# Two output projections with the high and the low part of the activations in one 512-column product

## What is computed

```python
for i in range(DEPTH):                       # 2 layers: RG-LRU mixer, then GLA mixer
    h = rmsnorm_2(x, norm_g[i, 0]) * (1.0 + sc_m) + sh_m
    y = rglru_mixer(h, ...) if i == 0 else gla_mixer(h, ...)    # ends in  ... @ w_out   (1024 x 1024)
    x = x + gt_m * rmsnorm_2(y, norm_g[i, 1])
    h = rmsnorm_2(x, norm_g[i, 2]) * (1.0 + sc_f) + sh_f
    y = conv_ffn(h, ...)                     # ends in  ... @ w_down  (2816 x 1024)
    x = x + gt_f * rmsnorm_2(y, norm_g[i, 3])
```

## Time and profile before

| | |
|---|---|
| median of 3 runs | 1930.6 us (1929.88 to 1931.36) |
| profiled execution, its time | 1930.98 us |
| profiled execution, its span | 1929.2 us |
| instructions | 30067 |
| PE busy | 1847.6 us, 96% of the span |
| DVE busy | 1439.3 us, 75% |
| ACT busy | 887.6 us, 46% |
| HBM traffic | 157 GB/s on average |

### The profile page before, as it was taken

The page is one execution under the profiler, slowest core; times in us unless marked ns, Lnnn a source line. Parts: engine busy times, 40 slices in busy tenths (PEclk is TensorE's granted clock), DMA queues, the critical chain, the costliest instruction groups (busy, mean ns, idle before and its releaser), DMA issues.

```text
span 1929.2 us, 30067 instructions
## 1 busy us (share of the span) xinstructions
PE 1847.6 (96%) x11558; PEld 1619.9 (84%) x11558; DVE 1439.3 (75%) x2531; ACT 887.6 (46%) x1523; POOL 0.2 (0%) x4
## 2 busy tenths in 40 slices
PE   5899999999999999999999999999999999999997
PEld 2688887767888887988878999987999979989997
DVE  5548866558789897797866887676888778768863
ACT  3322223456232333443456455574655355546552
POOL 0000000000000000000000000000000000000000
PEclk9999999999999999999999999999999999999999
DMA  9333222011767777443222996443556924225552
GB/s 343 101 92 105 88 88 66 23 34 57 250 233 255 242 240 260 127 142 126 88 68 66 308 311 211 132 143 110 196 177 237 331 73 146 88 92 193 191 164 82
DMA packets 242909, 302.78 MB, mean 157 GB/s; under 512 B 6080, under 2 KB 224448, under 8 KB 242256
## 3 DMA queue, kind: packets, MB, share of 16 engines
q1 hardware_dynamic: 242768, 300.87, 47.1%
HBM read 299.79 MB, written 1.05 MB: 156 GB/s over the span
## 4 chain that ended last, share of the span: by engine, by line
PE 81%; DVE 8%; ACT 6%; issue 2%; SPq 1%; DMA 1%; DVEq 0%; ACTq 0%
PE bank L514 25%; PE bank L515 24%; PE bank L516 24%; DVE w_lo L1713 1%; ACT w_hi L1095 1%; PE bank L763 1%; DVE work L2150 1%; ACT work L1081 1%; PE bank L947 1%; PE bank L751 1%; PE bank L734 1%; PE bank L492 1%; PE bank L860 1%; DMA arena<-in_w_mod 1%; DVE arena L1781 1%
## 5 line engine op out<-in xcount | busy, mean ns | idle before, releaser
L514 PE MATMUL bank<-h_hi,w_hi 128*128 128x256 f32 (+2 forms) x2800 | 893.5, 319 | 27.5 <-DVE h_lo L1659 11.2
L515 PE MATMUL bank<-h_lo,w_hi 128*128 128x256 f32 (+2 forms) x2800 | 882.2, 315 | 0.0
L516 PE MATMUL bank<-h_hi,w_lo 128*128 128x256 f32 (+2 forms) x2800 | 881.6, 315 | 0.0
L1713 DVE TENSOR_TENSOR w_lo<-ring,w_hi 128x1024 fp32r<-128x1024 f32 (+2 forms) x444 | 500.3, 1135 | 232.9 <-ACT w_hi L1095 227.1
L514 PEld LDWEIGHTS bank<-h_hi,w_hi 128*128 128x128 f32 x2800 | 532.1, 190 | 78.9 <-ACT h_hi L1175 17.2
L516 PEld LDWEIGHTS bank<-h_hi,w_lo 128*128 128x128 f32 x2800 | 532.9, 190 | 35.5
L515 PEld LDWEIGHTS bank<-h_lo,w_hi 128*128 128x128 f32 x2800 | 531.3, 190 | 35.2 <-issue 0.7
L1095 ACT ACTIVATE w_hi<-ring 128x1024 fp32r<-128x1024 f32 (+2 forms) x444 | 434.4, 985 | 183.9 <-PE bank L516 152.3
L1081 ACT ACTIVATE work<-bank 128x512 f32<-128x512 f32 (+1 forms) x150 | 73.4, 506 | 306.6 <-PE bank L516 262.1
L514 PE MATMUL bank<-arena_r,w_hi 128*128 128x256 f32 (+2 forms) x464 | 154.0, 332 | 3.5 <-issue 1.9
L1081 ACT ACTIVATE arena<-bank 128x256 f32<-128x256 f32 (+4 forms) x113 | 51.4, 455 | 219.3 <-PE bank L516 156.9
(11 more groups left out here) (241 smaller groups left out, 1568.8 us busy)
## 6 DMA issues: line engine op xcount, KB each, us to landing
ring<-in_w_in SPq DMA_DIRECT2D x86, 1024.0 KB, 5.4
arena<-in_ada_w_t SPq DMA_DIRECT2D x96, 512.0 KB, 6.2
ring<-in_ffn_w_up SPq DMA_DIRECT2D x44, 1024.0 KB, 5.1
ring<-in_w_branch SPq DMA_DIRECT2D x32, 512.0 KB, 4.8
arena<-in_w_mod_t SPq DMA_DIRECT2D x32, 512.0 KB, 5.5
ring<-in_ffn_w_down SPq DMA_DIRECT2D x16, 1024.0 KB, 5.5
ring<-in_gla_w_in SPq DMA_DIRECT2D x12, 1024.0 KB, 5.5
ring<-in_w_out SPq DMA_DIRECT2D x8, 1024.0 KB, 5.2
```

Source lines behind the costliest of these rows:

```text
L514: pe.matmul(out, ws[0][:, k, :], hi, start=start, stop=False)
L515: pe.matmul(out, ws[0][:, k, :], lo, start=False, stop=False)
L516: return pe.matmul(out, ws[1][:, k, :], hi, start=False, stop=stop)
L1713: step(nc.vector.tensor_tensor(w_lo[u % PARTS][:, 0:nk, :], src, w_hi[u % PARTS][:, 0:nk, :].bitcast(F32), ALU.subtract), f"lo {u}", *(["u ...
```

## The change

High and low activations, two tensors before, become halves of one (`h_both`, and `ff_both` for the input tiles 16 to 21 of the down projection), so that one access pattern names both parts of a tile: 2 x 256 columns. `wide_products` replaces `three_products` in the four products named above. Its first product multiplies the high weight with both parts in 512 columns, which fill the whole bank: columns 0 to 255 hold high by high, columns 256 to 511 high by low. Its second product adds low weight by high activation to the first half. The two halves must then be added, which DVE does in `whole`: yT = yT + bank[:, 256:512], after ACT has copied the first half. ACT squares `yT` afterwards (`square_y`), in its program one tile later than the copy.

```diff
--- before.py
+++ after.py
@@ -146,7 +146,9 @@
         params, tables = sbuf("params", N_PARAM), sbuf("tables", N_TABLE)
         xT = sbuf("xT", KT * 2 * S)[:].rearrange("p (t s) -> p t s", t=KT)
-        h_parts = [sbuf(n, KT * (2 * S + 4), F32R)[:].rearrange("p (t s) -> p t s", t=KT) for n in ("h_hi", "h_lo")]
+        h_both = sbuf("h_both", 2 * KT * (2 * S + 4), F32R)[:].rearrange("p (w t s) -> p w t s", w=2, t=KT)
+        h_parts = [h_both[:, i] for i in range(2)]
+        both_at = 2
         h_hi, h_lo = (h[:, :, 2:2 + 2 * S] for h in h_parts)
         g_hi, g_lo = (h[:, :, 0:LATE_N] for h in h_parts)
@@ -255,8 +257,17 @@
         zT, scan_one = carve(17408, S), carve(17664, S)
         ff_act = carve(4096, FT, S)
-        ff_hi, ff_lo = (arena_r[:, c:c + (FT - 2 * KT) * S].rearrange("p (t s) -> p t s", s=S)
-                        for c in (9728, 9728 + (FT - 2 * KT) * S))
+        ff_both = arena_r[:, 9728:9728 + 2 * (FT - 2 * KT) * S].rearrange("p (w t s) -> p w t s", w=2, s=S)
+        ff_hi, ff_lo = ff_both[:, 0], ff_both[:, 1]
+
+        def ff_pair(n):
+
+            if n >= 2 * KT:
+                return ff_both[:, :, n - 2 * KT, :]
+            return h_both[:, :, n, both_at + S:both_at + 2 * S] if n < KT else h_both[:, :, n - KT, both_at:both_at + S]
+
+        def y_pair(n):
+            return h_both[:, :, n, both_at + S:both_at + 2 * S]
         def ff_part(h, n):
@@ -515,6 +526,11 @@
                 pe.matmul(out, ws[0][:, k, :], lo, start=False, stop=False)
                 return pe.matmul(out, ws[1][:, k, :], hi, start=False, stop=stop)
+            def wide_products(out, ws, k, hi, both, start, stop):
+
+                pe.matmul(out[:, 0:2 * S], ws[0][:, k, :], both, start=start, stop=False)
+                return pe.matmul(out[:, 0:S], ws[1][:, k, :], hi, start=False, stop=stop)
+
             def both_parts(name):
                 def ready(k):
                     pe.wait_ge(*scalar.did(f"hi {name}.{k}"))
@@ -840,8 +856,8 @@
                             for k in range(k0, min(k0 + 8, FT)):
                                 if c == 0 and j == 0:
                                     both_parts(f"ff {l}")(k)
-                                m = three_products(outs[j][:, 0:S], parts, k - k0, ff_part(h_hi, k), ff_part(h_lo, k),
-                                                   k == 0, k == FT - 1)
+                                m = wide_products(outs[j], parts, k - k0, ff_part(h_hi, k), ff_pair(k),
+                                                  k == 0, k == FT - 1)
                             done = [f"filled y {tag}.{2 * c + j}"] if k == FT - 1 else []
                             m.then_inc(*tensor.does(parts[2], *done))
                     for j in range(2):
@@ -863,9 +879,21 @@
             def block_out(tag, ready):
-                project_group([f"y {tag}.{n}" for n in range(GROUP)], S, ready, part(h_hi, S), part(h_lo, S))
+                names = [f"y {tag}.{n}" for n in range(KT)]
+                ws = [unit(name) for name in names[:GROUP]]
+                outs = [open_bank(name) for name in names[:GROUP]]
+                for k in range(KT):
+                    ready(k)
+                    for name, w, out in zip(names, ws, outs):
+                        m = wide_products(out, w, k, h_hi[:, k, S:2 * S], y_pair(k), k == 0, k == KT - 1)
+                        if k == KT - 1:
+                            m.then_inc(*tensor.does("filled " + name, w[2]))
                 for n in range(GROUP, KT):
-                    project(f"y {tag}.{n}", S, part(h_hi, S), part(h_lo, S))
+                    w = unit(names[n])
+                    out = open_bank(names[n])
+                    for k in range(KT):
+                        m = wide_products(out, w, k, h_hi[:, k, S:2 * S], y_pair(k), k == 0, k == KT - 1)
+                    m.then_inc(*tensor.does("filled " + names[n], w[2]))
                     for m in range(GROUP) if n == GROUP else (n - 1,):
                         sum_y(tag, m)
                 sum_y(tag, KT - 1)
@@ -1462,9 +1490,17 @@
                 name = f"y {tag}.{k}"
                 act.wait_ge(*tensor.did("filled " + name))
-                nc.scalar.activation(yT[:, k, :], bank(name)[:, 0:S], ACT.Copy)
-                nc.scalar.activation(sq8[:, k, :], bank(name)[:, 0:S], ACT.Square)\
-                    .then_inc(*scalar.does(name, "emptied " + name))
+                nc.scalar.activation(yT[:, k, :], bank(name)[:, 0:S], ACT.Copy).then_inc(*scalar.does("half " + name))
+                if k:
+                    square_y(tag, k - 1)
+                if k == KT - 1:
+                    square_y(tag, k)
+
+            def square_y(tag, k):
+
+                name = f"y {tag}.{k}"
+                act.wait_ge(*vector.did("whole " + name))
+                nc.scalar.activation(sq8[:, k, :], yT[:, k, :], ACT.Square).then_inc(*scalar.does(name))
             def block_out(tag, src, ready):
@@ -2254,12 +2290,21 @@
                         after(f"yn {tag}.{k}")
                         step(nc.vector.tensor_tensor(xT[:, k, 0:S], xT[:, k, 0:S], yT[:, k, :], ALU.add), f"x {tag}.{k}")
+            def whole(tag, k):
+
+                name = f"y {tag}.{k}"
+                dve.wait_ge(*scalar.did("half " + name))
+                step(nc.vector.tensor_tensor(yT[:, k, :], yT[:, k, :], bank(name)[:, S:2 * S], ALU.add),
+                     "whole " + name, "emptied " + name)
+
             def block_parts(tag, src, l):
                 first_units(f"y {tag}.0")
                 for n in range(KT):
                     low_part(f"{tag}.{n}", h_lo[:, n, S:2 * S], src[:, n, :], h_hi[:, n, S:2 * S])
-                split_to(unit_of[f"y {tag}.{KT - 1}"])
+                for n in range(KT):
+                    split_for(f"y {tag}.{n}")
+                    whole(tag, n)
                 post(tag, l, 1)
             def ffn(l):
@@ -2307,6 +2352,11 @@
                         split_to(unit_of[f"down {l}.{c}.{8 * i}.1"])
                         if l == 0:
                             mod_blocks(mod_plan[2, DOWN * c + i])
+                        if c and i == 0:
+                            for j in range(2):
+                                whole(f"ffn {l}", 2 * c - 2 + j)
+                for j in range(2):
+                    whole(f"ffn {l}", KT - 2 + j)
                 if l == 0:
                     modulation2(1)
                     settled()
@@ -2385,7 +2435,9 @@
             for k in range(KT):
                 step(nc.vector.scalar_tensor_tensor(xT[:, k, 0:S], xT[:, k, 0:S], param("fin_w")[:, k:k + 1],
                                                     stat2[:, 0:S], ALU.mult, ALU.mult), f"x fin.{k}")
-            split_to(unit_of[f"y rg.{KT - 1}"])
+            for n in range(KT):
+                split_for(f"y rg.{n}")
+                whole("rg", n)
             post("rg", 0, 1)
             ffn(0)
```

## The result

The changed kernel takes 1938.64 us (median of 6 runs, 1934.76 to 1942.95) against 1930.93 for the kernel before (6 runs, 1929.88 to 1932.89): a ratio of 1.004 with an interval of 1.0024 to 1.0056, so 4.6 to 10.8 us slower. The profiled execution took 1939.69 us with a span of 1937.8, 8.6 more than the span of before. The forecast was 1942.8, in a range of 1937.5 to 1949: the direction holds, the size is 4 us too large.

The account below looks back on a forecast made before the run. TensorE's stream of products was taken to bound the kernel. Terms 2.7 + 5.7 + 0.65 + 3.0 + 1.6 + 0.7 - 2.1 = 12.25 us on the profiled 1930.98 gave 1943.2, or 1942.8 from the median; range 1937.5 to 1949.

Parts of the forecast that it names:

- the sums inside the mixer outputs: After y.4, y.5, y.6 in both mixer outputs, TensorE's sums wait for ACT's square: 6 x 0.95 = +5.7 us.
- the ends of the mixer outputs: Last product to sum takes 1.71 us against 1.03, because of the addition: 0.68 us at each end.
- tile 4 after y.3: First mixer output: addition of y.0 stands behind the final norm, so tile 4 starts later: +3.0 us.
- the low clock behind it: First mixer output, products after the wait ahead of tile 4 run near 1.2 GHz: +1.6 us, bounds 0 and 3.
- the waits are shorter: Rival: only the ends (2.7) and 2 to 4 us elsewhere against 3.9 saved: 1931.5 to 1933.5 us; chance 0.06.
- the clock stays low: Rival: waits keep 1.2 GHz through y.4 to y.7 of both mixer outputs, +16.8 us, 1959.6; chance 0.12.
- The ends of the two down projections: Costed like the mixer outputs' ends: addition between copy and square adds 0.68 us at each.
- The saving per pair: Wide plus narrow product 0.353 us against 0.361 for three: 0.008 us each, 480 pairs, at most 3.9 us.
- the sum of the four stages: Both mixer outputs and both down projections: forecast terms add up to 12.25 us.
- The rival in which the product counts as a whole: Weight load isn't hidden, so a removed product saves up to 0.1204 us: about 1903 us; chance 0.03.
- The first down projection: Unit 1.8.0 starts 1.7 us later, 116 pairs save 0.9: +0.7 us without its end, +1.4 by stage.
- The step that failed: Residual and norm behind each mixer output: forecast 0 difference, no term for the split_for look-ahead.

Follow-up runs that it names:

- Experiments 3 and 4: Changed kernel with ACT's square of tile n-1 ahead of its wait for tile n: 1931.43 us; changed kernel with final norm behind the addition of y.3: 1930.38 us.
- Experiment 1: Changed kernel, but VectorE splits no unit beyond that of y.7 in the mixer outputs, as before the change: 1945.62 us, ratio 1.0072.
- experiment 2: Kernel before the change with only the look-ahead added, three more units split ahead of the update of x: 1925.49 us, ratio 0.9964.

## Why the prediction was right, and where its size was off

**The waits** held, each near its size: the sums inside the mixer outputs 1.05 us behind the last product for a forecast 1.07, the ends of the mixer outputs +0.62 for +0.68, tile 4 after y.3 +3.3 for +3.0, the low clock behind it 1.5 us for an assumed 1.6. Experiments 3 and 4 take the first and the last two of these away and return 5.9 and 6.8 us by stage. The rival "the waits are shorter" falls with them, and so does "the clock stays low", since the granted clock is back at 1317.1, before tile 4 ends, and the waits behind y.4 to y.6 don't lower it. (That rival's text puts one or two slow tiles at 1946 to 1950; by its own 2.3 us a tile they would give 1945.1 to 1947.4.)

**Two terms were mis-sized.** The ends of the two down projections were put at 0.68 us each and are 0.35 and 0.34: the chain was read at a mixer output, and "nothing else is left to do there" doesn't hold where the sums of four tiles stand at the end. The saving per pair was put at 0.008 us and is 0.009: the second down projection has 1.59 us less to its last product over 176 pairs, and 1.24 less in all. The two errors have the same sign and make about 1 us. The sums inside the mixer outputs (six tiles at 1.04 us for 0.95) and tile 4 of the first one (+0.3) err the other way by about as much, so that the sum of the four stages came out closer than its terms.

The rival in which the product counts as a whole needed 0.041 per pair. A weight load that takes its turn with the products, as the Trainium skill has it in the place cited in the prediction, would have made 51 us by the estimate given there; 480 x 0.009 is 4.3. The same section of the Trainium skill also lets a load run ahead when it goes to a background weight buffer, and the measured pitch fits that case.

**The first down projection** came out near its sum (+1.2 for +1.4). As this stage varies by more than that from one execution to the next, the closeness of the sum is in part luck; the late low part isn't. Timeline of DVE, then of PE:

```profile
1501.05 1.29 DVE L1821 CUSTOM_DVE_ANT_0 arena<-arena,c_row,params 128x1024 f32<-128x1024 f32 x1 [0.70 <-DMA arena<-in_ada_w_t]
...
1503.57 0.75 DVE L2297 TENSOR_TENSOR arena<-arena,bank 128x256 f32<-128x256 f32 x2
1505.42 2.36 DVE L1749 TENSOR_TENSOR w_lo<-ring,w_hi 128x1024 fp32r<-128x1024 f32 x2 [1.10 <-ACT w_hi L1123]
```

```profile
1499.37 0.47 PE L531 MATMUL bank<-h_both,w_hi 128*128 128x512 f32 x1 [2.36 <-DVE w_lo L1749]
...
1506.79 0.47 PE L531 MATMUL bank<-h_both,w_hi 128*128 128x512 f32 x1 [1.54 <-DVE w_lo L1749]
```

The additions stand behind the blocks, at 1503.57, where before the low part of unit 1.8.0 stood; this low part follows at 1505.42 and TensorE starts the unit at 1506.79 behind a wait of 1.54. From the start of the stage (1472.70 before, 1480.89 after) that is 25.90 us against 24.03: +1.87 for a forecast of +1.7. The end adds 0.34 and the 116 pairs in between save 1.03, which makes the measured 1.18. One thing was not foreseen: the stretch at low clock of the earlier trace rows is missing after, and the time reappears one unit later as the wait of 2.36 at 1499.37, because the low part there is bound by the blocks in either kernel (16.68 us from the start of the stage before, 17.11 after). Experiment 1, with the same code here, has the low clock and starts that unit at 18.34 us behind a wait of 0.40, where the changed kernel starts it at 18.48 behind the 2.36. Clock lost ahead of a wait cost nothing here.

**The step that failed** is one that isn't in the sum, and it is worth more than the 4 us by which the size was off. The part on the change costs the additions of the new loop over y.0 to y.7 and nothing for its other call, split_for, as if it were the split_to that it replaces. But it looks three units further. So three of four low parts of the ffn's first units move from a place where TensorE waits for DVE to one where DVE waits for TensorE: 2 x 2.66 us, and the second time also the 1.2 us of low clock that stood behind TensorE's wait of 2.1 us. Experiment 1 takes this away (+7.0 us), experiment 2 gives it to the old kernel (-5.6). Without it the change would have cost 14.6 us (1945.62 against 1931.07), where 12.25 were forecast. By stage the four stages of the sum give 12.5 of that in experiment 1, and 1.5 more are in the first up projection (138.42 against 136.90), where the low clock stood in experiment 1 and not in the one profile of before. With the credit of 5.3 us for the two norms in the sum, the forecast would have been 1937.5, at the very edge of its range, and 1936.3 with the clock's 1.2. So the direction was understood, but that the result lies inside the range is in part luck.

**The front** is 2.1 us longer in the profile after, in code that wasn't changed, and within what it varies by from one execution to the next, as the last section shows.

## What to carry to other kernels

Merging two products into a wider one saved little here, where the weight loads already lie beside the products: read the pitch of both widths first (here 0.361 against 0.351 for the same columns), and then look at what the merge adds at every place where the result is waited for. Where an addition is put between a copy and its reader, check on each engine what stands in front of it: a square behind the next copy and an addition behind a norm cost over 12 us here, and other orders of the same work brought them back. An end is not like every other end: where TensorE still has sums to make, an addition between copy and square cost half of what it cost elsewhere. When a call in a loop replaces another, compare what both issue, not only what the line was written for: a look-ahead of three units was worth 5.6 us, more than the 4.3 that the 480 removed products can save.
